# Slot path first behind the branch, casts and gates in another order, a two-product residual and a last norm in two steps

## The chip, the core and the metric

The kernel runs on one core of a Trainium2 chip. The metric is the device time of one execution in microseconds (us). Three executions of the kernel before took 1161.95, 1162.05 and 1162.21 us, so the median is 1162.05 us.

## What is computed

The reference is a first block (modulation vectors from a condition, a SwiGLU feed-forward, a mixer of pooling and dilated attention, a second feed-forward) and two layers of a second block. What the change touches is this:

```python
h = h + gt2 * token_mixing(u, ...)            # merged = g_pool*(y_pool@w_pool_branch) + g_attn*(y_attn@w_attn_branch)
                                              # ... return merged @ w_out
# each of the two layers of the second block:
mix = jnp.concatenate([ret_o, swa_o, mla_o], -1) @ w_out[l]
x = layer_norm(DEEPNORM_ALPHA * x + mix, ln1_g[l], ln1_b[l])
x = layer_norm(DEEPNORM_ALPHA * x + grouped_moe(x, router_w, router_bias, w_gate_up[l], w_down[l]), ln2_g[l], ln2_b[l])
# grouped_moe: a group of 4 of the 16 experts per token, 2 experts within it; SwiGLU experts of width 256
```

There are 256 tokens of width 1024, as two token tiles (t = 0, 1) of 128.

## The kernel before

Every product of float32 values is made of three float16 products: a value is split in a high part and a low part, and hi*hi, hi*lo and lo*hi are added in PSUM (`split_mm`, L750). Weights come in *units* of 128x2048 float32 values (1 MB) through a ring of six: the sync engine (SP) loads `raw`, ScalarE (ACT) makes `whi` (L445), VectorE (DVE) makes `wlo` (L470), TensorE (PE) uses both. A load waits until the low part of the unit six places before is made; a high part waits until PE has used the unit six places before. ACT and DVE run ahead of PE by an order that is written out by hand: `unit`, `unit1`, `ahead` and `emit` stand between the other work of each engine, and each engine works strictly in its written order. SP too takes its loads in order, so a load that waits holds back all loads behind it.

*The mixer of the first block.* In `branch`, PE makes the two branch products for a quarter j of the columns; DVE multiplies them with the gates and adds them (L2571, L2574, L2576), ACT makes the high part of the sum (L1963), DVE the low part (L2578). Then come four units of the output product, in `last_downs` token tile by token tile; after each token tile DVE adds to x (L2261), ACT takes the square sums, and eight transposes (L888) lead to the second feed-forward, whose first step is `stage1_by_tokens`.

*The attention part of a layer* ends with `residual(t)`: ALPHA*x is added to the sum in PSUM by 24 products with scaled identity matrices (L906), three for each of 8 column tiles.

*The expert part of a layer.* The router chooses one of four groups for each token. If no group has more than 96 tokens, each group's tokens are gathered in 96 slots (`sparse`), otherwise all tokens go through all experts (`dense`). The count is made by DVE (`ranks`, semaphore `rank_out`), every engine loads it in a register and branches; the text of `dense` stands first, that of `sparse` behind it. In `sparse`, PE gathers the first group (L1522; ACT and DVE copy the result, `gather`), and then for each expert c does the first product in the slots (`slots_in_half`), and two experts later the second (`slots_down`). Between the experts 0 and 3 stand the gates in slots (L1678), the other gathers and the residual; after each group of four, `scatter` brings the rows back (L1690). Experts in `WHOLE` have their second weight unsplit: 4 float32 products of two passes each (L1642) take the place of 12 float16 products, no cast is needed, and SP loads the weight in one of two buffers (`x_flat`, `gt_flat`) in turn. The weight number i of them waits until that number i-2 has been used (`whole_used`).

`stay_warm(n, bank)` lets PE do n products with zeros, whose results nobody reads.

## Time and profile before

| | us |
|---|---|
| median of three executions | 1162.05 |
| profiled execution, its own time | 1163.61 |
| profiled execution, span from first to last instruction | 1161.8 |
| PE busy | 1106.2 (95%) |
| DVE busy | 879.8 (76%) |
| ACT busy | 629.2 (54%) |

The stages of the span: first block until about 589 us (branches and output product from 362 to 401, second feed-forward from 407), attention part of layer 0 until 709, its expert part until 866, then the same for layer 1; the stages of layer 1 lie 285.07 us behind those of layer 0 (the products with zeros that start at 724.49 in layer 0 start at 1009.56 in layer 1). The last output lands at 1161.8.

A busy PE says little, since the time of a product overlaps with that of the next. What the order of the work waits for is read from the idle time before an instruction (in brackets, with what ended it) and from the chain that ended last.

### The profile page before, as it was taken

Reading aid. Unit: us, or ns where it says so; the run is one execution under the profiler, and the core shown is the slowest. Engines: PE = TensorE matmul, PEld = TensorE weight load, DVE = VectorE, ACT = ScalarE, POOL = GpSimd, SP = SyncE. Lnnn points to the kernel's source line nnn. Section 1 sums busy time; section 2 is a strip of 40 time slices with the busy share of each in tenths; the row PEclk is TensorE's granted clock in tenths of the full one; section 3 lists DMA queues with packets and bytes.
Section 4 is the critical chain, followed back from the end, with each engine's and each line's share of the span. In section 5 each row is a group of like instructions: output and inputs, shape, how many; then the busy total and the mean of one; then the engine's idle time right before and its main releaser. Section 6 shows DMA issues by size and latency. Waiting matters only on the chain.

```text
span 1161.8 us, 25234 instructions
## 1 busy us (share of the span) xinstructions
PE 1106.2 (95%) x10870; PEld 850.9 (73%) x10870; DVE 879.8 (76%) x1109; ACT 629.2 (54%) x782; POOL 90.2 (8%) x104
## 2 busy tenths in 40 slices
PE   4899999999999899999999999999999999999995
PEld 4777776698787487777688785887759777588772
DVE  4799799789775775556667857999956775799994
ACT  1554344453465554344466446777746644677762
POOL 1115511071000100000000000000000000000000
PEclk9799999899999999999999999999999999999997
DMA  9999799466544577665464225599985333479970
GB/s 341 371 369 374 245 351 357 145 223 201 187 167 161 171 251 267 217 217 154 141 199 148 75 72 222 206 383 407 381 264 168 112 109 99 194 279 387 399 317 36
DMA packets 134430, 271.95 MB, mean 234 GB/s; under 512 B 9396, under 2 KB 98072, under 8 KB 126008
## 3 DMA queue, kind: packets, MB, share of 16 engines
q1 hardware_dynamic: 123960, 231.79, 56.4%
q0 software_dynamic: 7904, 29.25, 7.1%
q10 hardware_dynamic: 2464, 9.44, 2.1%
q8 instruction: 78, 1.28, 0.5%
q14 instruction: 24, 0.20, 0.0%
HBM read 269.41 MB, written 1.05 MB: 233 GB/s over the span
## 4 chain that ended last, share of the span: by engine, by line
PE 72%; DVE 14%; ACT 7%; DMA 4%; issue 3%; ACTq 0%; SPq 0%; DVEq 0%
PE ps L750 57%; DVE wlo L470 7%; ACT whi L445 2%; DMA area<-in_w_ada_dram 2%; PE ps L1642 2%; DMA raw<-in_w_in_dram 1%; PE ps L888 1%; PE ps L1238 1%; PE ps L1268 1%; PE ps L906 1%; PE ps L1278 1%; DVE x L2262 1%; PE ps L1522 1%; PE ps L1075 1%; PE ps L1267 1%
## 5 line engine op out<-in xcount | busy, mean ns | idle before, releaser
L470 DVE SCALAR_TENSOR_TENSOR wlo<-raw,whi 128x2048 f16<-128x2048 f32 (+4 forms) x212 | 466.1, 2231 | 49.2 <-ACT whi L445 48.4
L445 ACT ACTIVATE whi<-raw 128x2048 f16<-128x2048 f32 (+4 forms) x212 | 384.6, 1848 | 26.2 <-DMA raw<-in_w_ffn_in_dram 10.2
L750 PE MATMUL ps<-uhi,whi 128*128 128x256 f16 (+2 forms) x1328 | 330.8, 261 | 0.9 <-DVE ulo L2317 0.4
L750 PE MATMUL ps<-ulo,whi 128*128 128x256 f16 (+2 forms) x1328 | 330.6, 261 | 0.0
L750 PE MATMUL ps<-uhi,wlo 128*128 128x256 f16 (+2 forms) x1328 | 330.5, 261 | 0.0
L750 PE MATMUL ps<-whi,hreg 128*128 128x512 f16 (+1 forms) x656 | 204.8, 381 | 0.2 <-DVE area L2897 0.2
L750 PE MATMUL ps<-area,whi 128*128 128x96 f16 (+2 forms) x2168 | 154.9, 210 | 3.2 <-ACT area L2157 3.2
L750 PEld LDWEIGHTS ps<-area,whi 128*128 128x128 f16 (+2 forms) x2168 | 145.4, 99 | 15.4 <-issue 9.0
L750 PE MATMUL ps<-area,wlo 128*128 128x96 f16 (+2 forms) x1084 | 149.4, 210 | 0.0
L750 PEld LDWEIGHTS ps<-uhi,whi 128*128 128x128 f16 (+1 forms) x1328 | 130.8, 98 | 23.4 <-issue 9.0
L750 PEld LDWEIGHTS ps<-ulo,whi 128*128 128x128 f16 (+1 forms) x1328 | 130.6, 98 | 15.4 <-issue 1.7
L750 PEld LDWEIGHTS ps<-uhi,wlo 128*128 128x128 f16 (+1 forms) x1328 | 130.6, 98 | 11.9
L750 PE MATMUL ps<-wlo,hreg 128*128 128x512 f16 (+1 forms) x328 | 124.8, 381 | 0.0
L750 PEld LDWEIGHTS ps<-whi,hreg 128*128 128x128 f16 (+1 forms) x656 | 69.0, 105 | 70.6 <-issue 2.9
L750 PEld LDWEIGHTS ps<-area,wlo 128*128 128x128 f16 (+2 forms) x1084 | 107.3, 99 | 0.0
L2358 DVE SCALAR_TENSOR_TENSOR area<-area,cond 128x512 f32 (+1 forms) x94 | 72.0, 766 | 11.8 <-DMA area<-in_w_ada_dram 8.8
L1811 ACT ACTIVATE hreg<-ps 128x512 f32<-128x512 f32 x22 | 13.1, 597 | 117.1 <-PE ps L750 117.1
L750 PEld LDWEIGHTS ps<-wlo,hreg 128*128 128x128 f16 (+1 forms) x328 | 34.5, 105 | 33.7 <-issue 2.2
L2324 DVE SCALAR_TENSOR_TENSOR hreg<-ps,hreg 128x512 f32<-128x512 f32 x22 | 15.1, 688 | 46.5 <-ACT hreg L1811 46.5
L550 POOL DMA_DIRECT2D area<-in_w_ada_dram x48 | 34.9, 727 | 162.9 <-DVE area L2358 130.9
L1813 ACT ACTIVATE hreg<-hreg 128x512 f16<-128x512 f32 x22 | 13.9, 630 | 57.9 <-DVE hreg L2324 57.9
L2005 ACT ACTIVATE xn<-ps,x 128x128 f32<-128x128 f32 (+1 forms) x48 | 19.7, 416 | 41.9 <-DVE x L2631 24.7
(361 smaller groups left out, 1428.0 us busy)
## 6 DMA issues: line engine op xcount, KB each, us to landing
raw<-in_exp_w_gate_up_dram SPq DMA_DIRECT2D x64, 1024.0 KB, 7.6
raw<-in_w_ffn_in_dram SPq DMA_DIRECT2D x44, 1024.0 KB, 7.3
raw<-in_w_in_dram SPq DMA_DIRECT2D x34, 1024.0 KB, 7.1
area<-in_w_ada_dram POOLq DMA_DIRECT2D x48, 512.0 KB, 7.3
raw<-in_w_ffn_out_dram SPq DMA_DIRECT2D x22, 1024.0 KB, 8.0
raw<-in_exp_w_down_dram SPq DMA_DIRECT2D x22, 1024.0 KB, 7.8
raw<-in_w_out_dram SPq DMA_DIRECT2D x12, 1024.0 KB, 5.5
x<-in_exp_w_down_dram SPq DMA_DIRECT2D x6, 1024.0 KB, 5.5
```

The costliest lines, as they stand in the source:

```text
L445: act.activation(whi[:, u.slot, 0:n], raw[:, u.slot, 0:n], ACT.Copy, scale=SW)\
L470: dve.scalar_tensor_tensor(out=wlo[:, u.slot, 0:n], in0=raw[:, u.slot, 0:n], scalar=SW, in1=whi[:, u.slot, 0:n], op0=ALU.mult, op1=ALU.sub ...
L550: eng.dma_start(aring[:, j, :, :], w_ada[:, 2 * j:2 * j + 2, c0:c0 + ADA_BLOCK]).then_inc(ada_late[j], 16)
L750: last = pe.matmul(o, st, mv, start=start and i == 0, stop=stop and i == 2, skip_group_check=True)
L888: ins = pe.transpose(ps[:, 4 + 2 * t + k // 4, (k % 4) * P:(k % 4 + 1) * P], xn[:, t, k * P:(k + 1) * P], ident)
L906: pe.matmul(o, st[:, k, xs], mv, start=k % 4 == 0 and i == 0, stop=False, skip_group_check=True)
L1642: last = pe.matmul(ps[0:SLOTS, 6 + n, :], e_whole[i % 4][:, f * SLOTS:(f + 1) * SLOTS], whole[i % 2][:, f * D + n * HALF:f * D + (n + 1) * ...
L1811: act.activation(s_act, ps[:, 4 + 2 * par, :], ACT.Silu, scale=1.0 / S).then_inc(silu_made, 1)
L1813: act.activation(hhi[:, par, :], h_f32, ACT.Copy).then_inc(h_hi, 1)
L2005: last = act.activation(sb2[h % 2][:, SPLIT[t]], ps[:, 2 + h % 2, SPLIT[t]], ACT.Exp, scale=scale_of(h), bias=st[:, 1, t:t + 1], accum_out ...
L2324: dve.scalar_tensor_tensor(out=h_f32, in0=ps[:, 5 + 2 * par, :], scalar=SX / S, in1=s_act, op0=ALU.mult, op1=ALU.mult).then_inc(h_made, 1)
L2358: ins = dve.scalar_tensor_tensor(out=v, in0=w, scalar=cond[:, k:k + 1], in1=v, op0=ALU.mult, op1=ALU.add)
```

## The change

1. *Experts.* `WHOLE` loses expert 14: its second weight is split like most others (one more unit in the ring), and expert 15 takes its buffer.
2. *Residual.* ALPHA goes out of the residual into the other operands: their scales are divided by ALPHA, the layer norm's epsilon by its square, and one exact factor (64) is left, so that `residual` has two products for each column tile instead of three.
3. *Branch.* On PE, `sparse` now stands first behind the compare and `dense` behind it. The products with zeros before the branch go from 20 to 6; 4 stand behind the first gather; the 8 that stood behind both paths become 9 at the end of `sparse` in layer 0.
4. *Before the branch.* ACT made four high parts and then copied the first gather; it makes one, copies, and makes three. DVE made the gates and then copied the gather; it copies first.
5. *Mixer.* The cast of one unit that DVE made before the four merges stands behind the second of them; ACT makes one high part behind its second merge that it made after the fourth.
6. *Second feed-forward.* Five products with zeros stand before the transposes of its token tile 1.
7. *Last norm.* (value - mean)*gain is made from PSUM while ACT makes the square root, then *rstd + bias, by half rows, each stored by itself.

```diff
-WHOLE = (3, 7, 11, 14, 15)
+WHOLE = (3, 7, 11, 15)
...
             for t in range(TT):
-                sp.wait_ge(x_new, 12 + t + 1)
-                sp.dma_start(out[0, t * P:(t + 1) * P, :], x[:, t, :]).then_inc(out_done, 16)
-            sp.wait_ge(out_done, 32)
+                for hf in range(2):
+                    c = slice(hf * HALF, (hf + 1) * HALF)
+                    sp.wait_ge(x_new, 12 + 2 * t + hf + 1)
+                    sp.dma_start(out[0, t * P:(t + 1) * P, c], x[:, t, c]).then_inc(out_done, 16)
+            sp.wait_ge(out_done, 64)
...
                                 pe.wait_ge(mod_cols, 4)
+                                if q == 1:
+                                    stay_warm(5, 7)
                                 token_transposes(q, 1)
...
-                    for i, (st, mv) in enumerate(((uhi, res_hi), (ulo, res_hi), (uhi, res_lo))):
-                        pe.matmul(o, st[:, k, xs], mv, start=k % 4 == 0 and i == 0, stop=False, skip_group_check=True)
+                    for i, st in enumerate((uhi, ulo)):
+                        pe.matmul(o, st[:, k, xs], res_one, start=k % 4 == 0 and i == 0, stop=False, skip_group_check=True)
...
-                stay_warm(20, 0)
+                stay_warm(6, 0)
...
                     first_gather()
+                    stay_warm(4, 7)
                     for c in range(EXPERTS):
...
                     scatter(3)
+                    if l < LAYERS - 1:
+                        stay_warm(9, 7)
...
-                with pe.If(count > SLOTS):
+                with pe.If(count < SLOTS + 1):
+                    sparse()
+                with pe.Else():
                     dense()
-                with pe.Else():
-                    sparse()
                 if l < LAYERS - 1:
-                    stay_warm(8, 7)
                     token_transposes(2 * l + 4, 0)
...
                                ACT.Copy).then_inc(m_hi, 1)
+                if j == 1:
+                    unit1(24)
...
-                emit(4)
+                emit(1)
                 gather(0)
+                emit(3)
...
-            unit1(23)
             for j in range(4):
...
                                   mhi[:, 2 * j:2 * j + 2, :], ALU.subtract).then_inc(m_lo, 1)
+                if j == 1:
+                    unit1(23)
...
+                gather(0)
                 gates()
-                gather(0)
                 emit(1)
...
             for t in range(TT):
-                dve.wait_ge(xn_made, 14 + t + 1)
-                dve.wait_ge(xa_made, 12 + t + 1)
-                link(dve.tensor_tensor(x[:, t, :], xn[:, t, :], lng, ALU.mult))
-                dve.tensor_tensor(x[:, t, :], x[:, t, :], lnb, ALU.add).then_inc(x_new, 1)
+                dve.wait_ge(var_made, 2 * (2 * LAYERS - 1) + t + 1)
+                for hf, c in enumerate(halves):
+                    ins = dve.scalar_tensor_tensor(out=x[:, t, c], in0=ps[:, 2 * t + hf, :], scalar=stat[:, 8 + 4 * t:9 + 4 * t],
+                                                   in1=lng[:, c], op0=ALU.subtract, op1=ALU.mult)
+                link(ins)
+            for t in range(TT):
+                dve.wait_ge(rms_made, 2 * (2 * LAYERS + 3) + t + 1)
+                link(dve.reciprocal(stat[:, 4 + t:5 + t], stat[:, 2 + t:3 + t]))
+                for c in halves:
+                    dve.scalar_tensor_tensor(out=x[:, t, c], in0=x[:, t, c], scalar=stat[:, 4 + t:5 + t], in1=lnb[:, c],
+                                             op0=ALU.mult, op1=ALU.add).then_inc(x_new, 1)
```

How the instructions stand in a row, at three places. First DVE at the merges of the mixer (`area<-ps` are the gated products, `wlo<-raw,whi` a cast), before:

```order
L2448 SCALAR_TENSOR_TENSOR hreg<-ps,hreg 64x256
L470 SCALAR_TENSOR_TENSOR wlo<-raw,whi 128x2048
L2571 SCALAR_TENSOR_TENSOR area<-ps,area 128x512
L2574 SCALAR_TENSOR_TENSOR area<-ps,area 128x512
L2576 TENSOR_TENSOR area<-area 128x512
L2578 TENSOR_TENSOR area<-area 128x512
L2571 SCALAR_TENSOR_TENSOR area<-ps,area 128x512
L2574 SCALAR_TENSOR_TENSOR area<-ps,area 128x512
L2576 TENSOR_TENSOR area<-area 128x512
L2578 TENSOR_TENSOR area<-area 128x512
L2571 SCALAR_TENSOR_TENSOR area<-ps,gt 128x512
```

And the same place of DVE now:

```order
L2459 SCALAR_TENSOR_TENSOR hreg<-ps,hreg 64x256
L2579 SCALAR_TENSOR_TENSOR area<-ps,area 128x512
L2582 SCALAR_TENSOR_TENSOR area<-ps,area 128x512
L2584 TENSOR_TENSOR area<-area 128x512
L2586 TENSOR_TENSOR area<-area 128x512
L2579 SCALAR_TENSOR_TENSOR area<-ps,area 128x512
L2582 SCALAR_TENSOR_TENSOR area<-ps,area 128x512
L2584 TENSOR_TENSOR area<-area 128x512
L2586 TENSOR_TENSOR area<-area 128x512
L470 SCALAR_TENSOR_TENSOR wlo<-raw,whi 128x2048
L2579 SCALAR_TENSOR_TENSOR area<-ps,gt 128x512
```

The cast has moved from ahead of the first merge to behind the second.

Second PE at the branch of a layer (`ps<-zeros,diag` are the products with zeros, `ps<-area 128x96` the gather), before:

```order
L1512 MATMUL ps<-area,small 128x8
L898 MATMUL ps<-zeros,diag 128x512 x20
L1726 TENSOR_LOAD area
L1727 COMPARE_AND_BRANCH
L1522 MATMUL ps<-area 128x96 x32
L1556 MATMUL ps<-diag,area 128x128 x32
```

And PE at the same place now:

```order
L1516 MATMUL ps<-area,small 128x8
L902 MATMUL ps<-zeros,diag 128x512 x6
L1733 TENSOR_LOAD area
L1734 COMPARE_AND_BRANCH
L1526 MATMUL ps<-area 128x96 x32
L902 MATMUL ps<-zeros,diag 128x512 x4
L752 MATMUL ps<-area,whi 128x96 x2
```

Before, what follows the compare is `dense` (its transposes, L1556); now it is the slot path, and `dense` has gone behind it, some 1180 rows further.

Third DVE at the end of layer 0's slot path (`hreg<-ps,hreg` and `hreg<-hreg,area` are the gated activation of an expert), from expert 14 on, before:

```order
L2911 SCALAR_TENSOR_TENSOR hreg<-ps,hreg 128x192
L2918 TENSOR_TENSOR hreg<-hreg,area 128x192
L470 SCALAR_TENSOR_TENSOR wlo<-raw,whi 128x2048
L470 SCALAR_TENSOR_TENSOR wlo<-raw,whi 128x1024
L470 SCALAR_TENSOR_TENSOR wlo<-raw,whi 128x2048
L2911 SCALAR_TENSOR_TENSOR hreg<-ps,hreg 128x192
L2918 TENSOR_TENSOR hreg<-hreg,area 128x192
L2897 SCALAR_TENSOR_TENSOR area<-ps,area 96x512 x2
```

And DVE at that end now:

```order
L2922 SCALAR_TENSOR_TENSOR hreg<-ps,hreg 128x192
L2929 TENSOR_TENSOR hreg<-hreg,area 128x192
L470 SCALAR_TENSOR_TENSOR wlo<-raw,whi 128x2048
L2936 TENSOR_TENSOR hreg<-hreg 128x192
L470 SCALAR_TENSOR_TENSOR wlo<-raw,whi 128x2048
L470 SCALAR_TENSOR_TENSOR wlo<-raw,whi 128x1024
L2922 SCALAR_TENSOR_TENSOR hreg<-ps,hreg 128x192
L2929 TENSOR_TENSOR hreg<-hreg,area 128x192
L470 SCALAR_TENSOR_TENSOR wlo<-raw,whi 128x2048
L2908 SCALAR_TENSOR_TENSOR area<-ps,area 96x512 x2
```

The first cast is now that of expert 14's second weight, and one cast of layer 1's units stands behind expert 15's activation instead of ahead of it.

## Rows read from the trace of the kernel before

**Rows 1.** Windows, expert part of layer 1: window, us, busy by engine (count), clock, DMA, GB/s.

```profile
1062.00:1092.00 30.00, 30.00 (x446) 23.20 (x443) 29.65 (x26) 23.52 (x22) 0.00 (x0) 1.00 1.01 401
```

**Rows 2.** Timeline, PE, first branch product: start, duration, engine, line, operation.

```profile
362.26 0.38 PE L750 MATMUL ps<-hreg,whi 128*128 128x256 f16 x2
```

**Rows 3.** Timeline, DVE, merges and what follows: in brackets the idle time before.

```profile
365.32 2.29 DVE L470 SCALAR_TENSOR_TENSOR wlo<-raw,whi 128x2048 f16<-128x2048 f32 x1 [5.13 <-ACT whi L445]
...
383.61 8.90 DVE L470 SCALAR_TENSOR_TENSOR wlo<-raw,whi 128x2048 f16<-128x2048 f32 x4 [2.62 <-ACT whi L445]
392.42 0.69 DVE L2261 TENSOR_TENSOR xn<-ps,gt 128x512 f32<-128x512 f32 x1
```

**Rows 4.** Timeline, ACT, the casts after the four merges.

```profile
381.69 7.29 ACT L445 ACTIVATE whi<-raw 128x2048 f16<-128x2048 f32 x4
```

**Rows 5.** Timeline, PE, transposes before the second feed-forward.

```profile
397.08 1.09 PE L888 MATMUL ps<-small,xn 128*128 128x128 f32 x8 [1.40 <-DVE xn L2275]
405.95 1.94 PE L888 MATMUL ps<-small,xn 128*128 128x128 f32 x8 [2.50 <-DVE xn L2275]
```

**Rows 6.** Windows, PE alone, behind the second transposes: busy (count), clock, DMA.

```profile
406.00:409.00 3.00, 3.00 (x21) 0.50 1.01 366
```

**Rows 7.** Chain in order of time: start, us, what; one residual of the attention part.

```profile
685.95 1.34 PE ps L906 x24
```

**Rows 8.** Timeline, PE, branch and first gather of layer 0; then the gathers of layer 1.

```profile
724.49 4.48 PE L898 MATMUL ps<-zeros,diag 128*128 128x512 f16 x20
729.85 1.52 PE L1522 MATMUL ps<-area 128*128 128x96 f16 x32 [0.89 <-issue]
733.00 0.20 PE L750 MATMUL ps<-area,whi 128*128 128x96 f16 x1 [1.62 <-ACT area L2157]
...
1033.03 0.39 PE L1522 MATMUL ps<-area 128*128 128x96 f16 x5 [0.66 <-issue]
...
1039.18 0.43 PE L1522 MATMUL ps<-area 128*128 128x96 f16 x6 [0.58 <-issue]
```

**Rows 9.** Timeline, DVE, from the count into the slot path, layer 0.

```profile
725.36 0.15 DVE L2815 CAST area<-area 128x1 int32<-128x1 f32 x1
...
741.27 0.36 DVE L2918 TENSOR_TENSOR hreg<-hreg,area 128x192 f32<-128x192 f32 x1 [1.08 <-ACT area L2208]
...
749.53 2.29 DVE L470 SCALAR_TENSOR_TENSOR wlo<-raw,whi 128x2048 f16<-128x2048 f32 x1 [0.60 <-ACT whi L445]
```

**Rows 10.** Timeline, ACT, ahead of the branch and the first copy in it.

```profile
725.22 7.30 ACT L445 ACTIVATE whi<-raw 128x2048 f16<-128x2048 f32 x4
...
737.73 1.02 ACT L2204 ACTIVATE area<-ps 96x1024 f16<-96x1024 f16 x1
```

**Rows 11.** Timeline, DVE's casts for experts 5 and 6, PE's first unsplit second product, layer 0.

```profile
765.54 6.69 DVE L470 SCALAR_TENSOR_TENSOR wlo<-raw,whi 128x2048 f16<-128x2048 f32 x3
...
775.75 3.64 PE L1642 MATMUL ps<-x,hreg 128*96 128x512 f32 x8
```

**Rows 12.** Chain in order of time: second products of one expert, unsplit and split.

```profile
1120.91 3.48 PE ps L1642 x8
...
1136.87 2.59 PE ps L750 x12
```

**Rows 13.** Timeline, SP's queue, end of layer 0's expert part.

```profile
838.36 0.37 SPq L612 DMA_DIRECT2D x<-in_exp_w_down_dram  x1
```

**Rows 14.** Timeline, PE, second product of expert 15 in layer 0.

```profile
857.58 3.67 PE L1642 MATMUL ps<-x,hreg 128*96 128x512 f32 x8 [0.74 <-DVE hreg L2918]
```

**Rows 15.** Timeline, the last norm on DVE, and the stores on SP's queue.

```profile
1149.17 0.21 DVE L2282 BATCH_NORM_AGGREGATE stat<-bnst 128x2 f32<-128x12 f32 x1
...
1150.79 1.42 DVE L2281 BATCH_NORM_STATS2 bnst<-ps 128x6 f32<-128x512 f32 x2
...
1157.52 1.23 DVE L2949 TENSOR_TENSOR x<-x,area 128x1024 f32<-128x1024 f32 x1
...
1156.37 2.75 SPq L631 DMA_DIRECT2D out_dram<-x  x2
```

More of the change, by code:

```diff
@@ L113, in constants @@
     small[:, C_EPSLN] = LN_EPS
-    small[:, C_EPSLN + 1] = LN_EPS * S * S
+    small[:, C_EPSLN + 1] = LN_EPS * S * S / (ALPHA * ALPHA)
     small[:, C_PRIO16:C_PRIO16 + 16] = 16 - np.arange(16)
@@ L205, in build @@
         bnst = sb("bnst", [P, TT, 12])
-        diag = sb("diag", [P, 3, P], F16)
+        diag = sb("diag", [P, 2, P], F16)
         rbias = sb("rbias", [P, 16])
@@ L309, in build @@
         earlier, slot_no = cosb2[:, 0:P], cosb2[:, P:T]
-        ident16, res_hi, res_lo = diag[:, 0, :], diag[:, 1, :], diag[:, 2, :]
+        ident16, res_one = diag[:, 0, :], diag[:, 1, :]
         tk = region(area[:, 3328:15360])
@@ L1061, in _ @@
             ada_ones(0, range(8))
-            pe.wait_ge(diag_made, 3)
+            pe.wait_ge(diag_made, 2)
             transposes(0)
@@ L1964, in _ @@
                                ACT.Copy).then_inc(m_hi, 1)
+                if j == 1:
+                    unit1(24)
             act.activation(flag[:, 6:7], zero8[:, 0:1], ACT.Sqrt)
-            for i in range(24, N_MIX):
+            for i in range(25, N_MIX):
                 unit1(i)
@@ L2013, in pair_hi @@
                     act.wait_ge(xo_mm, 6 * l + p + 1)
-                    act.activation(mixhi[:, 2 + p, :], ps[:, 6, 0:T], ACT.Copy, scale=SX).then_inc(yo_hi, 1)
+                    act.activation(mixhi[:, 2 + p, :], ps[:, 6, 0:T], ACT.Copy, scale=SX / ALPHA).then_inc(yo_hi, 1)
                 def mla_query(j):
@@ L2116, in _ @@
                 act.wait_ge(ret_t, l + 1)
-                act.activation(mixhi[:, 0:2, :], ps[:, 7, :].rearrange("p (k n) -> p k n", k=2), ACT.Copy, scale=SX)\
+                act.activation(mixhi[:, 0:2, :], ps[:, 7, :].rearrange("p (k n) -> p k n", k=2), ACT.Copy,
+                               scale=SX / ALPHA)\
                     .then_inc(ret_hi, 1)
@@ L2193, in group_out @@
                         act.activation(ysh[g % 2][0:SLOTS, n * HALF:(n + 1) * HALF], ps[0:SLOTS, 6 + n, :], ACT.Copy,
-                                       scale=SX / S).then_inc(ys_hi[l], 1)
+                                       scale=SX / (S * ALPHA)).then_inc(ys_hi[l], 1)
                 def sparse():
@@ L2234, in _ @@
                     token_std(2 * l + 1, t)
-                    token_norm(2 * l + 1, t)
+                    if l < LAYERS - 1:
+                        token_norm(2 * l + 1, t)
                     if l < LAYERS - 1 and t == 0:
@@ L2457, in _ @@
             dve.wait_ge(const_in, 32)
-            unit = np.float32(ALPHA * S / SX)
-            hi = np.float16(unit)
-            for i, value in enumerate((1.0, float(hi), float(np.float16(unit - np.float32(hi))))):
+            for i, value in enumerate((1.0, S / SX)):
                 dve.tensor_scalar(diag[:, i, :], ident, value, None, ALU.mult).then_inc(diag_made, 1)
@@ L2656, in pair_lo @@
                     dve.wait_ge(yo_hi, 4 + 6 * l + p + 1)
-                    dve.scalar_tensor_tensor(out=mixlo[:, 2 + p, :], in0=ps[:, 6, 0:T], scalar=SX, in1=mixhi[:, 2 + p, :],
+                    dve.scalar_tensor_tensor(out=mixlo[:, 2 + p, :], in0=ps[:, 6, 0:T], scalar=SX / ALPHA, in1=mixhi[:, 2 + p, :],
                                              op0=ALU.mult, op1=ALU.subtract).then_inc(yo_lo, 1)
@@ L2760, in _ @@
                 dve.wait_ge(ret_hi, l + 1)
[L2761 removed]
+                dve.scalar_tensor_tensor(out=mixlo[:, 0:2, :], in0=ps[:, 7, :].rearrange("p (k n) -> p k n", k=2), scalar=SX / ALPHA,
                                          in1=mixhi[:, 0:2, :], op0=ALU.mult, op1=ALU.subtract).then_inc(ret_lo, 1)
@@ L2882, in dense @@
                         h = d_whole[WHOLE.index(c) % 2] if keep else d_h
-                        dve.scalar_tensor_tensor(out=h, in0=ps[:, 5 + 2 * (c % 2), :], scalar=SX * SW / S if keep else SX / S,
+                        dve.scalar_tensor_tensor(out=h, in0=ps[:, 5 + 2 * (c % 2), :],
+                                                 scalar=(SX * SW if keep else SX) / (S * ALPHA),
                                                  in1=d_act, op0=ALU.mult, op1=ALU.mult).then_inc(e_m, 1)
@@ L2938, in _ @@
                 token_stats(2 * l + 1, 0)
-                token_norm(2 * l + 1, 0)
                 if l < LAYERS - 1:
+                    token_norm(2 * l + 1, 0)
                     token_split(4, 0, vec8[:, V_LN2G:V_LN2G + 8], vec8[:, V_LN2B:V_LN2B + 8])
                 token_stats(2 * l + 1, 1)
-                token_norm(2 * l + 1, 1)
+                if l < LAYERS - 1:
+                    token_norm(2 * l + 1, 1)
             dve.wait_ge(last_in, 32)
+            halves = [slice(0, HALF), slice(HALF, D)]
             for t in range(TT):
-                dve.wait_ge(xn_made, 14 + t + 1)
-                dve.wait_ge(xa_made, 12 + t + 1)
-                link(dve.tensor_tensor(x[:, t, :], xn[:, t, :], lng, ALU.mult))
-                dve.tensor_tensor(x[:, t, :], x[:, t, :], lnb, ALU.add).then_inc(x_new, 1)
+                dve.wait_ge(var_made, 2 * (2 * LAYERS - 1) + t + 1)
[9 more added lines that the diff above has]
+                                             op0=ALU.mult, op1=ALU.add).then_inc(x_new, 1)
 _INS = ["x", "c", "positions", "w_ada", "b_ada", "g_norm_ffn1", "w_ffn1_in", "w_ffn1_out", "g_norm_mix", "w_in", "w_pool",
```

3 lines of the change are left out of this document (1 added, 2 removed).

## The prediction

> **What bounds the kernel now.** I read the windows first, then the idle times on PE, DVE and ACT in the timeline, then the chain of waits. In the expert part PE has no idle time, DVE is busy 29.65 us of 30, ACT 23.5, and the DMA engines are full [rows 1]: PE sets the pace and DVE stands just behind it. So a product that goes is worth its time there, and an earlier start of PE is worth what DVE and ACT can follow. Elsewhere the places that matter are those where PE stands still: the merges of the mixer, where DVE waits 5.13 us for a high part [rows 3]; the transposes of the second feed-forward, reached after 2.50 us of idle time and done at half the clock [rows 5, 6]; the entry of the slot path [rows 8]; expert 15 of layer 0 [rows 14]; and the last norm, where DVE alone works [rows 15]. The long feed-forwards are PE without a gap and keep their length.
>
> All durations are of the profiled execution, whose own time is 1163.61 (span 1161.8); that is 1.56 above the median of 1162.05. I sum the differences, take them off 1163.61, and carry the same sum to the median.
>
> **Merges.** The first merge stands behind a cast that begins at 365.32 and takes 2.29, so it starts at 367.6 [rows 3]. What it really needs is the first pair of branch products: 24 products of 256 columns from 362.26 [rows 2], at 0.108 each (half of 2.59/12 for 512 columns [rows 12]), so 364.9. That is 2.7 earlier; the last idle time before it shrinks from 5.1 to what PE needs. The cast (2.2) now lies between merges two and three, so merges three and four gain only 0.5. After the fourth, DVE's casts began at 383.61 after 2.62 of waiting for ACT, hence merge four ended at 381.0 and now ends at 380.5. The first of its four casts has its high part made long before and runs 380.5 to 382.7. The other three follow ACT, whose casts began at 381.69 and take 1.82 each [rows 4]: from 381.2, first done 383.05, then three low parts of 2.22: 389.7. The addition to x began at 392.42 [rows 3]: 2.7 earlier. PE is ready for it: two branch pairs till 367.5, seven products with zeros 369.0, two pairs 374.2, two units of 24 products 384.6, then 12 products each for two units till 389.8, the first half row done at 388.5. The path from the addition to the transposes is unchanged: 405.95 becomes 403.25.
>
> Before these transposes PE idles 2.50 and its clock is then 0.50, that is 1.2 GHz instead of 2.4, until a little after 409 [rows 5, 6]. After 1.40 of idle time eight such transposes took 1.09, not 1.94. Five products with zeros (1.1) leave 1.4 of idle time, so I expect the full clock: 0.85 on the transposes and half of the 1.4 us from 407.9 on, 0.7. Sum of this place: 2.7 + 0.85 + 0.7 = 4.2; from there PE has no gap. If the clock still falls: 2.7.
>
> **Residual.** 24 products in 1.34 are 0.056 each [rows 7]. 8 go for each token tile, 16 at each of four places: 0.9 each. In the attention parts they lie in a run of PE work without idle time (the chain passes through them); the values behind them need a copy of DVE that is due 0.5 earlier too, so it doesn't come late. 2 x 0.9 = 1.8. In the expert parts the same: 1.8.
>
> **Entry of the slot path.** The count is there at 725.5 [rows 9], the gather starts at 729.85 [rows 8]: 4.3 for the register load, the compare and the jump over `dense`, most of it hidden beneath 20 products with zeros. Without the jump the gather comes between 726.7 (six products end at 725.8, and 0.89 idle as now) and 729.85 (all of it is the load). I take 727.0, near the first, since the jump is the only long step in it. By the Trainium skill (Runtime: NRT & Kernel Launch, Instruction fetch mechanics) a taken branch whose target lies outside the prefetched window forces a fetch of the target; the trace agrees so far as 4.3 is far more than a load and a compare should need. By its figures in Advanced Engine Details and Errata, Control Flow Timing, a compare-and-branch is about 0.11; the sum would then be larger by at most 0.3 a layer, since the zeros end at 725.8.
>
> Then: gather 1.4, till 728.4; four products with zeros 0.9; first expert from 729.2 (before 733.0 [rows 8]), 96 products at 0.043, till 733.4. ACT: one cast till 727.05 (7.30/4 = 1.83 [rows 10]), the copy with the gather till 728.5, three casts till 734.0, activation 0.3, and the copy of L2204 at 734.35 instead of 737.73 [rows 10]: 3.4 earlier. From this copy hang the gates in slots and expert 1, so PE moves by 3.4, not by 3.8. DVE does the same work in another order: its two casts for expert 1 end near 737.4 as before, and PE asks for them at 738.7. DVE loses only its idle times, 1.08 and 0.60 [rows 9], so it comes 1.7 earlier, PE with its residual 4.3. The narrowest place is expert 5: its casts ended at 767.7 and 769.9, PE needed the first at 775.75 - 4.1 = 771.6 [rows 11]. 3.9 of cover less 2.6 leaves 1.3. After it DVE is a little faster per group than PE. So 3.4 per layer, 6.8.
>
> **Expert 14.** 3.48 becomes 2.59 on PE [rows 12]: 0.9 per layer, 1.8. It costs DVE 2.2 + 0.3 and ACT 1.8 + 0.3. In layer 0 these fall where DVE waited for transfers: the load of expert 15's weight stood in SP's queue till expert 11 was used, 838.36 [rows 13], and all loads of layer 1 behind it. Now it waits for expert 7 only. So the activation of expert 15, which PE awaited for 0.74 [rows 14], comes in time: 0.7. In layer 1 nothing is queued behind it.
>
> **Leaving the slot path.** PE now jumps over `dense` at the end. The jump is issued with the last scatter, 3.2 before the transposes. The entry bounds it by 4.3 less the load: between 0 and 1.1 late; I take 0.3. In layer 1 PE stood 0.66 and 0.58 for its instructions during the gathers [rows 8], in layer 0 not. With the path straight ahead this may vanish (-1.2) or come in layer 0 as well (+1.2): I take -0.6. Together -0.3.
>
> **Last norm.** The first tile's aggregate is made at 1149.4, the second's statistics began at 1150.79 [rows 15]; they now follow directly and end with their aggregate at 1151.05. Four half rows at 0.61 (1.23/2): 1153.6. Twice a reciprocal 0.2 and two half rows: 1156.4, against 1157.52 + 1.23 = 1158.75. 2.3; the last store begins then, took 3.05 for 512 KB, and 256 KB can gain up to 0.3: I take 0.1. Sum 2.4. Four stores at 0.4 of SP each lie beneath.
>
> **Sum.** 4.2 + 1.8 + 1.8 + 6.8 + 1.8 + 0.7 + 0.3 + 2.4 = 19.8. 1163.6 - 19.8 = 1143.8; of the median, 1142.3.
>
> **Rivals.**
> - *The load, not the jump, is the 4.3.* The gather stays at 729.85; ACT's three casts come behind it (till 736.7) and L2204 at 737.1: 0.6 per layer instead of 3.4, so 5.6 less, 1147.9. For it: no row splits the 4.3. Against it: a load of one word is short beside it.
> - *DVE becomes the bound.* PE then follows DVE, which comes 1.7 earlier instead of PE's 4.3, in both layers: 5.2 less, 1147.5. For it: 29.65 of 30 [rows 1]. Against it: the cover of 3.9 [rows 11].
> - *Slower: code that runs dry.* The two stands of layer 1 are 6.15 apart. If in the new layout each such stretch of both slot paths (some 136 us each, 44 stretches) costs 0.62 while the DMA engines are full, that is 27 us, and 1162.05 + 27 - 19.8 = 1169. It decides from 32 such stands on. Against it: there were two, both within 25 us of a jump.
>
> **How the numbers follow.** Forecast 0.66; load 0.14; DVE 0.16; slower 0.02; the rest 0.02 is no change, if several of these and the lower clock meet. The forecast's own range is 1139.5 to 1145. Both middle rivals together give about 1149, and the bounds of unknown costs on the other side (fetch 1.2, branch 0.6, store 0.2, earlier DVE) 1139; range 1138.5 to 1149. Faster by over 0.2% (2.3 us, what a measurement of this kernel can tell from no change): 0.96; within 0.2%: 0.02; slower: 0.02.
>
> **What would show it.** Right: no idle time of 5 us before the first merge, the addition to x near 389.7; the transposes after it in 1.1; the first gather 1.5 behind the count; the first unsplit product of layer 0 at 775.75 - 4.2 - 0.9 - 3.4 - 0.9 = 766.3; no idle time before expert 15; DVE's end 7.0 behind the first tile's last aggregate. Wrong: DVE as releaser of PE inside the slot path; a gather 4 us behind the count; clock 0.50 after the warm products; casts of layer 1 that wait for transfers.

## Result and the profile after

The changed kernel takes 1148.78 us (median of 4, 1145.56 to 1150.89) against 1162.0: ratio 0.9895, 95% interval 0.9858 to 0.9931. It is faster, by 13.3 us and not by 19.8. The profiled execution has a span of 1147.1 instead of 1161.8, own time 1149.03 instead of 1163.61.

Executions of one kernel spread by several us, much of it ahead of the changed code: in the profiles of two experiments the mixer's end came 3.5 and 4.0 us earlier than here; in both the clock was full between 210 and 220 us, where the other profiles show 0.66 to 0.68. So I compare distances between marks in one profile. The marks: A, the transposes of the first token tile at the end of the attention part (709.31 before, 703.60 after; layer 1 994.39, 984.74); B, the first scatter; C, the third; D, the last. The *exit* is what lies behind D in layer 0, where TensorE now jumps over `dense`.

| stage | before | after | gain | forecast |
|---|---|---|---|---|
| start to the transposes at 225.44, ahead of the changed order | 225.44 | 224.76 | 0.68 | none |
| from there to the second feed-forward's long run | 192.17 | 188.05 | 4.12 | 4.2 |
| attention residuals (to A, both layers) | 291.70, 121.09 | 290.79, 120.20 | 1.80 | 1.8 |
| A to B, layer 0 | 81.01 | 78.59 | 2.42 | 4.3 |
| A to B, layer 1 | 81.98 | 80.28 | 1.70 | 4.9 |
| C to D, layers 0, 1 | 12.17, 11.19 | 10.34, 10.34 | 2.68 | 2.5 |
| D to the second tile's transposes, layer 0 | 12.21 | 13.40 | -1.19 | -0.3 |
| D to the end, layer 1 | 15.64 | 13.13 | 2.51 | 2.4 |

The gains add up to 14.7, the difference of the spans. The forecasts are the prediction's terms, with the residual of the expert part and the fetch stands put where they fall; they add up to 19.8. The 0.68 is not the change's: these transposes lie between 220.7 and 226.1 in the profiles of all kernels, with the change or without it. So the change itself gains 14.0 in this profile, 5.8 less than forecast: 5.1 of that (9.2 - 4.1) lies between A and B, 0.9 at the exit, and the other stages give 0.2 more than forecast.

The timeline of TensorE after, layer 0 and then layer 1 (start, duration, engine, line, operation; in brackets the idle time before and its releaser):

```profile
720.64 1.52 PE L1526 MATMUL ps<-area 128*128 128x96 f16 x32 [0.41 <-DVE area L2830]
722.86 0.25 PE L752 MATMUL ps<-area,whi 128*128 128x96 f16 x2
765.24 3.64 PE L1646 MATMUL ps<-x,hreg 128*96 128x512 f32 x8
775.52 0.39 PE L752 MATMUL ps<-whi,hreg 128*96 128x512 f16 x1 [2.56 <-DVE area L2908]
...
1046.38 3.64 PE L1646 MATMUL ps<-x,hreg 128*96 128x512 f32 x8
1056.66 0.39 PE L752 MATMUL ps<-whi,hreg 128*96 128x512 f16 x1 [2.56 <-DVE area L2908]
```

They answer to [rows 8, 11]. TensorE did come early: the gather 3.5 us (17.04 behind A instead of 20.54), the first product 4.4, the first unsplit product 4.8. Then it stands 2.56 us, in each layer, before expert 4's second product, the first that writes the banks of group 0's sum again: VectorE must first have read the low part of that sum, group 0's output, out of them (L2908). The page gives the same as one group:

```profile
L752 PE MATMUL ps<-whi,hreg 128*128 128x512 f16 (+1 forms) x672 | 210.8, 383 | 5.1 <-DVE area L2908 5.1
```

The same product in the kernel before, a row that the prediction had not read:

```profile
783.64 0.39 PE L750 MATMUL ps<-whi,hreg 128*96 128x512 f16 x1 [0.17 <-DVE area L2897]
```

So TensorE was already 0.17 early there, and had no cover at all. The windows say why, before and after, from the count to that product (window, us, then busy time of PE, PEld, DVE, ACT and POOL, clock, DMA share, GB/s):

```profile
726.00:783.60 57.60, 54.72 (x978) 46.82 (x976) 54.73 (x72) 44.04 (x46) 0.00 (x0) 1.00 0.79 292
```

```profile
720.00:775.50 55.50, 51.90 (x954) 45.16 (x953) 54.68 (x73) 44.22 (x46) 0.00 (x0) 1.00 0.80 304
```

VectorE does the same 54.7 us of work in either window. From the count itself to the product, 58.13 us before and 55.72 after, it is busy for 55.22 and 54.86. What it could give back, 2.05 of idle time and 0.36 of busy time, is the gain of layer 0, 2.42.

In layer 1 the same 2.56 us cost more. The windows of after behind the wait, layer 0 and layer 1:

```profile
776.00:779.00 3.00, 3.00 (x32) 2.05 (x31) 2.96 (x4) 1.61 (x2) 0.00 (x0) 1.00 1.01 422
1057.00:1060.00 3.00, 3.00 (x10) 1.45 (x9) 2.97 (x5) 1.62 (x1) 0.00 (x0) 0.55 1.01 419
```

In layer 1 the clock fell to 1.2 GHz behind the idle time: 10 products instead of 32, and B comes at 80.28 and not 78.6, another 1.7. The two stands of [rows 8], 1.24 in all, are gone; before, A to B was 0.97 longer in layer 1 than in layer 0. So 1.70 is the gain of layer 1 (2.42 + 0.97 - 1.69).

The other terms. Chain after (start, us, what), to be held against [rows 3, 5]:

```profile
389.27 0.69 DVE xn L2272
...
402.71 1.09 PE ps L892 x8
403.80 8.04 PE ps L752 x144
```

The addition to x is 3.15 earlier, 2.47 of it by the change (forecast 2.7); the transposes take 1.09. VectorE still idles before the first merge, now for TensorE's products and no longer for a high part (timeline of VectorE):

```profile
364.49 0.69 DVE L2579 SCALAR_TENSOR_TENSOR area<-ps,area 128x512 f32<-128x512 f32 x1 [4.96 <-PE ps L752]
```

The exit after, where before the transposes stood 4.77 behind D and had 0.44 of idle time:

```profile
851.14 1.03 PE L1694 MATMUL ps<-area 96*128 96x512 f16 x4
852.71 1.04 PE L1694 MATMUL ps<-area 96*128 96x512 f16 x4 [0.54 <-DVE area L2908]
853.58 2.11 PE L902 MATMUL ps<-zeros,diag 128*128 128x512 f16 x9
857.08 1.09 PE L892 MATMUL ps<-small,xn 128*128 128x128 f32 x8 [1.39 <-issue]
```

And the last norm on VectorE, which answers to [rows 15]:

```profile
1136.98 0.21 DVE L2293 BATCH_NORM_AGGREGATE stat<-bnst 128x2 f32<-128x12 f32 x1
1137.11 1.38 DVE L2292 BATCH_NORM_STATS2 bnst<-ps 128x6 f32<-128x512 f32 x2
1138.52 0.21 DVE L2293 BATCH_NORM_AGGREGATE stat<-bnst 128x2 f32<-128x12 f32 x1
1138.65 2.82 DVE L2961 SCALAR_TENSOR_TENSOR x<-ps,stat,area 128x512 f32<-128x512 f32 x4
...
1143.22 1.42 DVE L2968 SCALAR_TENSOR_TENSOR x<-x,stat,area 128x512 f32<-128x512 f32 x2
```

It ends 7.45 behind the first aggregate (forecast 7.0, before 9.37); from there to the end of the last store it is 2.46 us instead of 3.05.

### The profile page after: what moved, and what is told of

Its sections match the earlier page's. It is cut to its first block, busy times and chain, and to the rows that moved or that the text cites. A ratio compares the mean times of both kernels' runs of the same rounds, so it can differ in the third digit from the quotient of the medians.

```text
span 1147.1 us, 25106 instructions
## 1 busy us (share of the span) xinstructions
PE 1097.5 (96%) x10800; PEld 845.6 (74%) x10800; DVE 882.8 (77%) x1112; ACT 631.2 (55%) x784; POOL 90.2 (8%) x104
## 4 chain that ended last, share of the span: by engine, by line
PE 76%; DVE 14%; ACT 4%; issue 3%; DMA 3%; ACTq 0%; DVEq 0%; SPq 0%
PE ps L752 62%; DVE wlo L470 6%; DMA area<-in_w_ada_dram 2%; PE ps L1646 2%; PE ps L1694 1%; PE ps L892 1%; PE ps L1242 1%; PE ps L1272 1%; DVE area L2853 1%; PE ps L1282 1%; ACT whi L445 1%; DVE x L2273 1%; PE ps L1271 1%; PE ps L1079 1%; DVE xn L2272 1%
## 5 line engine op out<-in xcount | busy, mean ns | idle before, releaser
L470 DVE SCALAR_TENSOR_TENSOR wlo<-raw,whi 128x2048 f16<-128x2048 f32 (+2 forms) x214 | 470.9, 2232 | 36.7 <-ACT whi L445 35.8
L445 ACT ACTIVATE whi<-raw 128x2048 f16<-128x2048 f32 (+2 forms) x214 | 388.3, 1848 | 19.4 <-DMA raw<-in_w_ffn_in_dram 9.3
L752 PE MATMUL ps<-whi,hreg 128*128 128x512 f16 (+1 forms) x672 | 210.8, 383 | 5.1 <-DVE area L2908 5.1
L752 PEld LDWEIGHTS ps<-whi,hreg 128*128 128x128 f16 (+1 forms) x672 | 71.4, 106 | 77.9 <-DVE hreg L2936 5.4
L752 PE MATMUL ps<-wlo,hreg 128*128 128x512 f16 (+1 forms) x336 | 128.7, 383 | 0.0
```

Source lines behind the costliest of these rows:

```text
L445: act.activation(whi[:, u.slot, 0:n], raw[:, u.slot, 0:n], ACT.Copy, scale=SW)\
L470: dve.scalar_tensor_tensor(out=wlo[:, u.slot, 0:n], in0=raw[:, u.slot, 0:n], scalar=SW, in1=whi[:, u.slot, 0:n], op0=ALU.mult, op1=ALU.sub ...
L752: last = pe.matmul(o, st, mv, start=start and i == 0, stop=stop and i == 2, skip_group_check=True)
```

## Experiments

The theory (V): VectorE's load between the count and group 0's output sets B, so what TensorE gains beyond 2.4 us is stood out at that product. The rivals: the missing part is TensorE's own (T: exit, clock, code), or ScalarE's (S). A to B is the measure, and "the wait" is TensorE's wait for group 0's output. Each distance below is from one profile. Ratios are to the kernel before.

**Low gather copies on ScalarE.**

```diff
+                def gather_low(g):      # ACT: the copies of VectorE's gather(g)
...
                         if c < 3:
                             gather(c + 1)
+                            gather_low(c + 1)
...
-                        if c < 3:       # DVE
-                            gather(c + 1)
```

> The changed kernel, with the six low copies of the gathers for groups 1 to 3 (2 x 0.47 us each, VectorE) moved to ScalarE. Theory V (VectorE is the bound at the entry): from the count to the low part of group 0's sum VectorE has no idle time, and TensorE waits 2.56 us for that part in each layer. VectorE loses 2.8 us of work ahead of it, so the wait is gone; layer 0 gains 2.5, layer 1 2.5 and the 1.7 that the lower clock behind the wait cost: about 6.5 us less than the changed kernel. Theory T (what is missing is TensorE's own: the jump at the exit, the clock, the code fetch): no change but for the clock, 0 to 2 us. Rival S (VectorE only follows ScalarE's casts): ScalarE has 2.8 us more, VectorE ends no earlier or later, 0 gain or up to 2 us of loss per layer.

Measured: 1142.23, ratio 0.9849 (0.9819 to 0.988), span 1141.1. A to B 76.66 and 76.64, full clock in both layers; the wait is 1.04 and 1.15. V holds, with a piece of S. The wait was to be gone and is not: VectorE lost 2.8 us of work but came only 1.9 earlier, and 0.8 of the difference is that ScalarE's cast for it was now late once (timeline of VectorE):

```profile
740.32 2.29 DVE L470 SCALAR_TENSOR_TENSOR wlo<-raw,whi 128x2048 f16<-128x2048 f32 x1 [0.79 <-ACT whi L445]
```

**A third residual product.**

```diff
+                    if third:
+                        pe.matmul(o, uhi[:, k, xs], zeros16[:, 0:P], start=False, stop=False, skip_group_check=True)
```

> The changed kernel, with the third residual product put back in the expert part alone, as a product with zeros (8 per token tile of 128 columns, 0.056 us each: 0.9 us per layer on TensorE, nothing on the other engines). Theory V: the 0.9 falls into the 2.56 us for which TensorE waits for VectorE later on: that wait becomes 1.7, the first scatter comes at the same distance from the attention's transposes (78.6 us in layer 0), the span stays within 0.3, or gets shorter if the clock of layer 1 then holds (1.7). Theory T: 0.9 per layer, 1.8 us longer.

Measured: A to B 78.58 and 78.57, the wait 1.66 in place of 2.56 in both layers.

```profile
775.70 0.39 PE L752 MATMUL ps<-whi,hreg 128*96 128x512 f16 x1 [1.66 <-DVE area L2910]
```

In layer 0 that is V to 0.01 us: there the saved product is worth nothing. In layer 1 the clock stayed full behind the shorter wait, and A to B is 1.7 shorter than in the changed kernel. But the kernel took 1153.17 (0.9937, 0.9916 to 0.9957), 4 us more than the changed one; the span was to stay or get 1.7 shorter, and that miss lies at the exit, where TensorE stood twice:

```profile
858.71 0.66 PE L892 MATMUL ps<-small,xn 128*128 128x128 f32 x4 [2.83 <-issue]
861.65 1.01 PE L892 MATMUL ps<-small,xn 128*128 128x128 f32 x4 [2.29 <-issue]
```

and the clock fell to 0.50; D to the second transposes is 18.96, against 13.40.

**Group 0's output one cast earlier.**

```diff
+                        if c == 5:
+                            group_out(0)
                         if c < EXPERTS - 1:
                             emit(1)
...
-                        if c in (5, 9, 13):
+                        if c in (9, 13):
```

(the same on ScalarE, ahead of its e_hi operation)

> The changed kernel, with group 0's two output operations (high part on ScalarE, low part on VectorE) put one cast earlier in the block of expert 5, 2.2 us and an e_lo operation of 0.27 ahead; no work is added or taken. Theory V, where the order at that one point is what binds: the wait of 2.56 shrinks to about 0.1 and nothing else is late: 2.4 in layer 0 and 2.4 + 1.7 (clock) in layer 1, 6 us shorter. Theory V2, where VectorE's whole load binds (it is 1.3 us later with the cast behind): TensorE waits next at a product that needs a cast, for 1 to 2.5 us, and the gain is 0 to 1.5 per layer. Theory T: no change, but for the clock.

Measured: 1147.45 (0.9896, 0.9869 to 0.9924). A to B is 76.09 and 76.10 without a wait, but the next group's low part is late:

```profile
800.89 0.39 PE L752 MATMUL ps<-whi,hreg 128*96 128x512 f16 x1 [1.86 <-DVE area L2910]
```

A to the second scatter is 107.43, in the changed kernel 107.90 (layer 0): of 2.5 us 0.5 stay. That is V2 in size, but not in place: TensorE was to wait for a cast and waits for the output of group 1. From the count (716.33) to that product (800.89) VectorE has no idle time that its timeline shows, 83.56 us busy of 84.56, so its load binds and not the place of group 0's output alone. Group 1's output was left behind its own cast; moving that too was not tried.

**The entry alone, and its halves.** Three kernels made from the one before: both halves, TensorE's branch with its products with zeros, and the order of ScalarE's and VectorE's work.

```diff
-                with pe.If(count > SLOTS):
-                    dense()
-                with pe.Else():
-                    sparse()
+                with pe.If(count < SLOTS + 1):
+                    sparse()
+                with pe.Else():
+                    dense()
```

```diff
-                emit(4)
+                emit(1)
                 gather(0)
+                emit(3)
...
-                gates()
                 gather(0)
+                gates()
```

> The kernel before, with the entry of the slot path alone changed (branch turned round, 6 and 4 products with zeros, ScalarE's first cast ahead of its gather copies and three behind, VectorE's gather ahead of its gates). Theory V: the first gather comes 3.5 us earlier and the first expert's products 4.4, but the first scatter only as far as VectorE does: 2.4 in layer 0 (from 81.0 us behind the attention's transposes to 78.6) and about 1.7 to 3.4 in layer 1, TensorE waiting 1.7 for VectorE; less 0.9 for the jump at the exit: 3 to 5 us shorter in all. Forecast as it stood: 3.4 per layer, 6.8 less 0.3. If the entry counted in full: 4.4 per layer, 8 us shorter.

> The kernel before with TensorE's branch turned round alone (and 6 and 4 products with zeros), without the new order of ScalarE's casts and VectorE's gather. Theory V: TensorE's first gather comes as early as with all of the entry, 3 us earlier than before, but ScalarE copies it only behind its four casts, which end where they did, so the first expert's products start 0.3 us earlier and the first scatter 0.3 to 0.6 earlier; with 1 to 1.7 us for the exit and 1.2 back from the two stands in layer 1: about no change, -1 to +1. Rival (the jump alone is the gain): 3 us earlier per layer, 5 us shorter in all.

> The kernel before with the other half of the entry alone: ScalarE's first cast ahead of its gather copies and three behind, VectorE's gather ahead of its gates; TensorE's branch, and its jump over the dense code, as before. Theory V (both halves are needed: the copies must be free and the gather early): the gather starts 20.5 us behind the attention's transposes as before, the copies follow it at once and the three casts behind them end at 736.7 (as before's numbers run), so the first scatter comes 0 to 0.8 earlier per layer: 0 to 1.5 us shorter in all. Rival O (the order is the whole gain and the branch did nothing): the first scatter at 78.6 in both layers as with both halves, 5 us shorter.

| kernel | us | ratio (95%) | A to B | wait for VectorE |
|---|---|---|---|---|
| before | 1162.0 | | 81.01, 81.98 | 0.17, none |
| both halves | 1158.38 | 0.9972 (0.9952 to 0.9992) | 78.56, 78.57 | 1.66, 1.66 |
| branch alone | 1166.56 | 1.0048 (1.0028 to 1.0068) | 82.62, 82.38 | 0.42, 0.43 |
| order alone | 1163.82 | 1.0014 (0.9993 to 1.0035) | 81.98, 81.74 | 1.45, 1.66 |

Both halves reach in layer 0 the 78.6 of the changed kernel, with three residual products, and in layer 1 too, since the clock stays full behind 1.66: V again. The branch alone was to change nothing and is slower, by A to B and by its exit (13.77 to the second transposes, before 12.21). Its gather comes 3.4 earlier, but ScalarE is in its four casts, so TensorE idles 4.16 instead of 1.62 and then runs at half the clock (timeline, then windows):

```profile
725.59 1.52 PE L1522 MATMUL ps<-area 128*128 128x96 f16 x32 [0.51 <-DVE area L2822]
732.14 0.24 PE L750 MATMUL ps<-area,whi 128*128 128x96 f16 x2 [4.16 <-ACT area L2159]
```

```profile
734.00:735.00 1.00, 1.00 (x16) 1.00 (x14) 1.00 (x2) 0.00 (x0) 0.00 (x0) 0.50 0.08 16
```

The order alone was to gain up to 1.5 and gains nothing: VectorE, put ahead of its gates to copy a gather that is still behind the jump, stands idle and is then late for group 0's output by 1.45 and 1.66 (timeline of VectorE):

```profile
729.20 1.24 DVE L2844 CAST area<-ps 128x384 f16<-128x384 f32 x2 [3.11 <-PE ps L1522]
```

Neither half gained time without the other.

**Without the five products with zeros in the mixer.**

```diff
-                                if q == 1:
-                                    stay_warm(5, 7)
```

> The changed kernel without its five products with zeros ahead of the second group of transposes of the mixer's end. Theory Z (the zeros hold the clock): TensorE idles about 2.5 us there again, the granted clock is 0.50 until some 3 us later, the transposes take 1.94 instead of 1.09 and the 144 products behind them 8.76 instead of 8.04: 1.6 us longer. Rival N (the clock fell in the kernel before for another reason, the half clock comes or goes by chance): the transposes still take 1.1, no change.

Measured: 1149.58 (0.9891, 0.986 to 0.9922), and the clock stayed:

```profile
403.15 1.06 PE L890 MATMUL ps<-small,xn 128*128 128x128 f32 x8 [2.50 <-DVE xn L2284]
```

With the same 2.50 us of idle time these transposes took 1.94 in the kernel before [rows 5], 1.94 in the profiles of both halves and of the order alone, 1.51 with the branch alone, and 1.06 here. In all nine profiles with the zeros, which leave 1.33 to 1.34 us of idle time, they took 1.09. So theory Z failed here, but four of five profiles without the zeros show slow transposes: behind 2.5 us of idle time the clock may fall or stay, and whether this layout needs the zeros is open.

**The exit.** Transposes and zeros written into both branches; apart from that, 48 products with zeros in the dense code, which never runs; and the changed kernel once more.

```diff
                     sparse()
+                    if l < LAYERS - 1:
+                        token_transposes(2 * l + 4, 0)
+                        stay_warm(9, 7)
```

```diff
                     gates()             # in dense()
+                    stay_warm(48, 7)
```

> The changed kernel with the token transposes behind the expert part and their nine products with zeros written into both branches, so that TensorE's jump over the dense code comes behind them and lies beside VectorE's and ScalarE's split. Theory J (the 1.39 us of idle time before these transposes are the jump, issued when TensorE has nothing behind it): from the last scatter to the transposes 4.8 us as in the kernel before instead of 5.9, and the product behind them still waits for VectorE alone: 1.0 to 1.2 us shorter. Rival C (code has to be fetched after any jump, and the fetch is longer than the 2.7 us beside it): the first product of the feed-forward starts late by 1 to 3 us, and the gain is nothing or a loss. With the third residual product (the run before) the exit stood 2.83 us and once more 2.29 us, so both are open.

> The changed kernel with 48 products with zeros more in TensorE's dense code, which never runs here: nothing is executed otherwise, only the code behind the exit lies further on. The exit stood at 5.9 us from last scatter to transposes (4.8 without a jump), and in other kernels at 5.6, 7.0 and 7.4, twice with a second stand behind it. Theory L (where the code lies sets the price of the jump): the exit changes by more than 0.3 us in either direction, from the 5.9 of the unpadded kernel. Theory C (it is the state of the moment): the padded and the unpadded kernel spread alike, by 0 to 3 us. Theory D (a jump costs about 1.1 us wherever it goes): 5.9 again.

> The changed kernel, nothing edited, a second profile of it on this chip. What the stages show every time is the kernel's own: theory V expects the wait of 2.56 us for the first low part in both layers and the first scatter at 78.6 us behind the transposes, plus 1.7 in neither, one or both layers if the half clock behind the wait comes by chance. Exit: 5.9 again if its price belongs to the kernel, another figure if it belongs to the moment. Ahead of the mixer's end another 3.4 us may be won or lost with the half clock between 210 and 220 us, as one profile has shown.

With the transposes inside, D to transposes is 4.78 as without a jump (J), but the feed-forward's first product, behind the jump, then stands 2.33 us that its row puts down to issue (C):

```profile
853.56 1.09 PE L892 MATMUL ps<-small,xn 128*128 128x128 f32 x8 [0.22 <-DVE xn L2303]
...
858.93 0.22 PE L752 MATMUL ps<-uhi,whi 128*128 128x128 f16 x1 [2.33 <-issue]
```

D to the second transposes: 14.17, worse than 13.40; the kernel 1150.18 (0.9909, 0.9883 to 0.9934). Padded: 13.50 and 1149.32 (0.9876, 0.9853 to 0.99); again: 13.34 and 1149.67 (0.989, 0.9874 to 0.9907). So the padding changed nothing (against L as it stands), the changed kernel repeats its own exit within 0.1, and the kernels that jump there lie between 12.41 and 18.96, against 12.21 of the two that don't. L isn't ruled out by that, since the padding lies behind the exit's jump. Kernels with one and the same TensorE program lie close: 13.01 to 13.58 (the changed kernel twice, low copies on ScalarE, early output), 13.77 and 13.86 (branch alone, both halves). Those whose TensorE program is another ahead of the exit lie apart: 15.55 without the five zeros, 15.03 with expert 14 whole, 18.96 with the third product, each with half clock in part of it. What sets the price is open. The repeated profile has the 2.55 us wait in both layers and, as the first, the half clock in layer 1 alone (A to B 78.58, 80.25).

**Expert 14 whole.**

```diff
-WHOLE = (3, 7, 11, 15)
+WHOLE = (3, 7, 11, 14, 15)
```

> The changed kernel with expert 14 done whole again, as in the kernel before (five weights unsplit instead of four). Theory as forecast: 0.9 per layer on TensorE, and in layer 0 expert 15's activation is late again by 0.7, because the load of its weight holds SyncE's queue until expert 11 is used: from the third scatter to the last 12.2 us in layer 0 and 11.2 in layer 1 instead of 10.3 in both, 2.8 us longer in all. Rival R (the split product adds 2.2 us to VectorE, which is the bound, so that its gain is lost elsewhere): the distances above still grow, but something else shrinks by as much; no place for it is seen, since VectorE has idle time behind the third group. Theory V says that the first scatter stays at 78.6 either way.

Measured: C to D 12.15 and 11.19 instead of 10.34 twice, 2.7 us, with expert 15's wait back in layer 0; A to B 78.57 in layer 0 and, with half clock behind the wait as in the changed kernel, 80.25 in layer 1. As forecast.

```profile
849.34 3.67 PE L1646 MATMUL ps<-x,hreg 128*96 128x512 f32 x8 [0.73 <-DVE hreg L2929]
```

The 2.8 us longer in all don't show in the time: 1149.33 (0.9884, 0.9867 to 0.99) against 1148.78, and either kernel's executions spread by more (4.6 and 5.3 us). The profiled execution's span is 4.1 longer, 1.6 of it at the exit.

**All reliefs together.** ScalarE's low copies behind the cast, the early output, the transposes inside the branches.

```diff
                         if 0 < c < EXPERTS - 1:
                             emit(1)
+                        if c < 3:
+                            gather_low(c + 1)
+                        if c == 5:
+                            group_out(0)
```

> The changed kernel with four edits: the low gather copies of groups 1 to 3 on ScalarE, each behind its next cast (ahead of it, VectorE waited 0.79 us for that cast); group 0's output operations one cast earlier; transposes inside the branches as in the run beside this one. Theory V2 (VectorE's load up to the second group's output binds, 2.56 us at the first and 1.86 at the second where the first is moved ahead): with 2.8 us less of work VectorE is in time at both, no wait of TensorE for the low part of any group, the first scatter 76.1 us behind the transposes and the second 105.4, against 78.6 and 107.9, both layers at full clock. With 1.1 for the exit: 2.5 + 4.2 + 1.1 = 7.8 us off the changed kernel's span of 1147.1. Rival S (ScalarE's load binds next): a wait of about 1 us per layer stays as in the run with the copies ahead of the cast, 6 us off.

Measured: 1141.21 (1140.96 to 1141.73), ratio 0.9832 (0.9806 to 0.9857), the lowest of all, though its interval overlaps that of the low copies on ScalarE alone (0.9849). From A in layer 0 to the end it is 8.2 us shorter than the changed kernel (the low copies alone: 5.9). A to B is 75.35 and 75.34 (forecast 76.1), to the second scatter 105.1 (forecast 105.4); no product waits for group 0's output, and only 0.30 us are left before the next group's (0.30 in layer 1 too); the clock stays full from A to C. The timeline of TensorE, then windows of layer 1, in which VectorE and TensorE stand level:

```profile
802.57 0.39 PE L752 MATMUL ps<-whi,hreg 128*96 128x512 f16 x1 [0.30 <-DVE area L2921]
```

```profile
1060.00:1090.00 30.00, 29.70 (x439) 22.94 (x437) 29.86 (x25) 23.97 (x22) 0.00 (x0) 1.00 1.01 410
```

D to the second transposes is 12.41 here, although TensorE's program is that of the 14.17 above: part of the price hangs on something outside of it.

## Why the prediction was wrong

Its direction stands, and its other terms came within 0.9 us each. The median, 1148.78, is 6.5 above the forecast of 1142.3 and lies at the upper end of the range named (1149), where the prediction had put both middle rivals together. Of the 19.8 us 5.1 are missing between A and B, and the step that failed there is one: "The narrowest place is expert 5 ... 3.9 of cover less 2.6 leaves 1.3". In its place the runs show that TensorE stands 2.56 us in each layer for VectorE's output of group 0, which had no cover at all.

- *Entry (forecast 6.8).* The part on TensorE was even too cautious: without the jump the gather starts 0.84 behind the count (719.80 to 720.64), not 1.5, and is released by VectorE's selection matrix; neither load nor code holds it. That rules out the first rival. By the Trainium skill (Runtime: NRT & Kernel Launch, Instruction fetch mechanics) a taken branch to a target outside the prefetched window forces a fetch; the trace agrees so far as the 4.3 between count and gather are gone with the jump, and it is the exit that now shows 1.39 of issue time; that a fetch fills this time no row shows. What failed is the cover. VectorE's casts were checked, but not the other thing that TensorE awaits from it, the output of group 0, whose cover in the kernel before was -0.17. PE was 4.8 early and stood 2.56. VectorE's idle times, which the prediction put at 1.08 and 0.60, were 2.04 with one of 0.36 that it left out; all three are gone.
- *Residual in the expert parts (1.8).* Worth 0 in layer 0, where the third product changed A to B by 0.01; in layer 1 the kernel with it was even 1.7 quicker to B, since its clock held. It was nearly right that TensorE has no idle time there before (0.17); it got some from the entry, and the 0.9 fell into it. Two gains on one engine were added that share one limit on another.
- *The rival "DVE becomes the bound"* is what happened. It had .16, and its price, 5.2 less, is close to the measured 5.1, which is luck in part: VectorE came 2.4 earlier, not 1.7, and the clock took 1.7 back in layer 1. Its own marker (VectorE as releaser inside the slot path) is the row that shows it. The slower rival did not come: no stand for code is left in the slot paths.
- *Merges (4.2): 4.1.* By the change the addition to x came 2.5 earlier (2.7 worked out), the transposes took 0.85 less and the products behind them 0.7 less, as forecast. That the zeros did this isn't shown: without them the clock stayed full as well. Of the signs, "no idle time of 5 us before the first merge" was ill chosen, since VectorE idles 4.96 there for TensorE.
- *Attention residual (1.8): 1.80. Expert 14 and 15 (2.5): 2.68*, each shown by the distances, the second by undoing it too. *Last norm (2.4): 2.51*, of which what follows VectorE's last operation, with the half-row stores, is 0.6, not 0.1, and VectorE 1.9, not 2.3.
- *Leaving (-0.3): -1.19.* The jump isn't hidden: it is 0.9 dearer, just above the upper bound named (1.1), and in other kernels much more. The two stands of layer 1, for which 0.6 was booked, did go, but what they gave back fell under the same limit of VectorE.

## What to carry to other kernels

Before an earlier start of one engine is booked as a gain, list every kind of thing that it awaits from the engine just behind it, the outputs and freed banks as well as the inputs, and take the least cover in the trace of before; a row with 0.17 us of idle time in brackets is that place. Gains on the same engine up to such a place don't add, they are cut at what the other engine can give. And a jump or a copy moved early pays only together with the engine that has to take it up: each half alone gained nothing or cost time.

## What the runs showed of the hardware

- Idle time of 2.5 us of TensorE may or may not be followed by half a clock. Behind the wait of 2.55 or 2.56 it fell to 1.2 GHz in 6 of 12 cases: layer 1 and not layer 0 in both profiles of the changed kernel, in the padded one and with expert 14 whole; both layers with the transposes inside the branches; neither without the five zeros. Each fall cost 1.7 us. Behind the waits of 1.04 to 1.66 us at this place it never fell (8 cases); behind 4.16 us it fell.
- With a jump over code that isn't run, the stage from D to the second transposes took 12.41 to 18.96 us, against 12.21 without one, half clock in part of the longest ones included. With one TensorE program it was 12.41 and 14.17, with another 13.01 to 13.58. 48 more products in the code jumped over did nothing (13.50).
